# A decoder step on one core: conditioning weights accumulated in PSUM at the start, and the retention's work spread over four engines

## The reference, cut to what matters

```
m = silu(c) @ w_mod + b_mod                      # 6 x 1024 columns, 9 conditioning rows
h = rmsnorm(x, norm1_w) * (1 + sc1) + sh1
z = h @ w_in                                     # rq rk rv rg (4 x 512), mq mk mv (3 x 512)
# retention, 8 heads of 64, chunks of 128 tokens, on rotary q and k
att = (q @ k.T) * dmat
o   = att @ v + (q @ s) * q_dec
s   = s * c_dec + (k * k_dec).T @ v
ret = silu(rg) * ((o - mean(o)) * rsqrt(var(o) + eps) * gn_w)
# block-sparse attention (MoBA): prompt over its own blocks, samples over 3 chosen cache blocks and their own
moba = rmsnorm per head(softmax(q k.T) v)
x = x + g1 * (concat(ret, moba) @ w_out)
x = x + g2 * ((silu(h2 @ w_gate) * (h2 @ w_up)) @ w_down)
```

## Time and profile before

| what | us |
|---|---|
| median of three runs (1113.23 to 1118.26) | 1115.62 |
| the profiled execution, its own time | 1118.47 |
| its span, first to last instruction | 1116.6 |
| PE busy | 979.4 (88%) |
| DVE busy | 656.7 (59%) |
| ACT busy | 339.4 (30%) |
| POOL busy | 91.0 (8%) |
| DMA moved 267.01 MB, mean | 239 GB/s |

### The profile page before, as it was taken

One profiled execution on the slowest core, in us unless ns is written; L12 is line 12 of the kernel. 1 busy time (PEld: TensorE's weight loads), 2 busy tenths in 40 slices (PEclk: granted clock), 3 DMA queues, 4 the chain that ended last, 5 costly groups with the idle time before them and its releaser, 6 DMA issues.

```text
span 1116.6 us, 20916 instructions
## 1 busy us (share of the span) xinstructions
PE 979.4 (88%) x7847; PEld 684.4 (61%) x7847; DVE 656.7 (59%) x1152; ACT 339.4 (30%) x678; POOL 91.0 (8%) x90
## 2 busy tenths in 40 slices
PE   3669999999999657467987699999999999999996
PEld 1356766766776334244753476767677777777775
DVE  3555775676676487776656657543266555553344
ACT  4331233324224324224214414333234222221113
POOL 0011110000010021101400123000000000000000
PEclk8679999999999788787988689999999999999998
DMA  9846878877777768576888567977847798887662
GB/s 294 303 150 232 309 252 280 294 263 265 272 261 261 229 229 307 189 257 208 267 300 281 188 212 249 276 226 227 272 123 216 193 233 236 226 242 237 202 227 80
DMA packets 220355, 267.01 MB, mean 239 GB/s; under 512 B 12785, under 2 KB 175929, under 8 KB 212066
## 3 DMA queue, kind: packets, MB, share of 16 engines
q1 hardware_dynamic: 111586, 123.21, 35.1%
q10 hardware_dynamic: 99456, 75.38, 22.0%
q0 software_dynamic: 9216, 67.11, 16.8%
HBM read 260.04 MB, written 5.64 MB: 238 GB/s over the span
## 4 chain that ended last, share of the span: by engine, by line
PE 73%; DVE 13%; DMA 5%; DVEq 3%; ACT 3%; issue 2%; SPq 1%; ACTq 0%
PE banks L1001 13%; PE banks L1002 12%; PE banks L1003 12%; PE banks L961 6%; PE banks L1016 4%; PE banks L1036 4%; PE banks L1091 4%; DVE KT L1638 4%; PE banks L1017 4%; PE banks L1018 4%; DMA raw<-in_w_mod 2%; PE banks L1179 2%; DVEq L1539 2%; DMA raw<-in_w_out 1%; PE banks L1164 1%
## 5 line engine op out<-in xcount | busy, mean ns | idle before, releaser
L1001 PE MATMUL banks<-ahi,whi 128*128 128x512 f32 x416 | 170.9, 411 | 0.0
L571 ACT ACTIVATE whi<-raw 128x1024 fp32r<-128x1024 f32 (+1 forms) x76 | 78.7, 1035 | 301.3 <-PE banks L1003 157.5
L1638 DVE STREAM_TRANSPOSE KT<-K 128x2048 f32<-128x2048 f32 x64 | 147.7, 2308 | 37.0 <-PE banks L1036 29.7
L1002 PE MATMUL banks<-alo,whi 128*128 128x512 f32 x416 | 164.2, 395 | 0.0
L1003 PE MATMUL banks<-ahi,rawlo 128*128 128x512 f32 x416 | 164.0, 394 | 0.0
L1601 DVE TENSOR_TENSOR rawlo<-raw,whi 128x1024 fp32r<-128x1024 f32 (+1 forms) x76 | 91.4, 1203 | 61.9 <-ACT whi L571 59.1
L478 POOL DMA_INDIRECT K<-in_cache_k,kidx x64 | 64.7, 1011 | 581.8 <-DVE KT L1638 538.2
L1001 PEld LDWEIGHTS banks<-ahi,whi 128*128 128x128 f32 x416 | 79.6, 191 | 31.5 <-issue 13.6
L1036 PE MATMUL banks<-KT,qbd 128*32 128x128 f32 x2048 | 75.2, 291 | 25.5 <-DVE KT L1638 24.2
L1016 PE MATMUL banks<-ahi,whi 128*128 128x512 f32 x224 | 93.6, 418 | 1.2 <-DVE rawlo L1608 0.9
L1003 PEld LDWEIGHTS banks<-ahi,rawlo 128*128 128x128 f32 x416 | 79.3, 191 | 17.7
(11 more groups left out here) (304 smaller groups left out, 1447.6 us busy)
## 6 DMA issues: line engine op xcount, KB each, us to landing
V<-in_cache_v SPq DMA_DIRECT2D x184, 256.0 KB
rawm<-in_w_mod ACTq DMA_DIRECT2D x15, 1024.0 KB
zT<-in_cache_v SPq DMA_DIRECT2D x52, 256.0 KB
raw<-in_w_in ACTq DMA_DIRECT2D x12, 1024.0 KB
raw<-in_w_gate ACTq DMA_DIRECT2D x22, 512.0 KB
raw<-in_w_up ACTq DMA_DIRECT2D x22, 512.0 KB
srw<-in_w_gate SPq DMA_DIRECT2D x22, 512.0 KB, 5.4
srw<-in_w_up SPq DMA_DIRECT2D x22, 512.0 KB, 6.7
```

What stands on the lines that cost most here:

```text
L571: act.activation(whi[t % 2][:, 0:kd, :], raw[u][:, 0:kd, t % 2 * P:(t % 2 + 1) * P], ACT.Copy).then_inc(s_hi, 1)
L1001: pe.matmul(out[:, :], whi[t % 2][:, k, :], hi(k), start=(first and n == 0), stop=False)
L1002: pe.matmul(out[:, :], whi[t % 2][:, k, :], lo(k), start=False, stop=False)
L1638: dve.transpose(KTb[:, :, :, :], Kb[g % 2][:, :]).then_inc(s_kt, 1)
```

## The change

**Start.** The first eight chunks of `w_mod` become eight pieces of two k by 1024 columns, with buffers of their own (`early`, the later `rawm` and `raw`), and x is loaded ahead of them. PE sums each half (four pieces) over k in PSUM in four column groups at once, so that DVE copies 128 x 256 once and adds the bias in two operations instead of folding. The halves are taken one after the other: the gains of k = 0 to 3 come from the first. Of the scaling of x by its root mean square two of four parts go to DVE. Tile 0 and half of tile 1 are placed before `keys(0)`; the order of `mod_chunk` moves one ahead, and the last no longer lies in slot 27.

**Retention.** The cosines, the decay of q and the scaling of three of the four pairs of heads go to POOL, in its queue between two gathers. Centring becomes a product with a matrix `centre` in place of the turning (the same operation on PE turns and centres). ACT squares straight from PSUM and stages the attention's heads; the squares of the attention's heads are accumulated by ACT unit by unit in slots 15 to 29 (32 small operations in all). PE makes k.v for each head alone, 64 columns wide, so that DVE runs the state at 128 rows. `turn_x` is spread, one a slot; the roots are taken one slot earlier. In slot 28 the values are turned earlier and the last unit's probabilities come behind the copies. `slot_rest` on PE is split in `slot_values` and `slot_tail`; their order in each slot comes out as in the kernel before (the tail's products ahead of `weigh` where s % 8 is 4, behind it elsewhere).

**Behind it.** Two waits in the first tile of the output projection move (`last_in`), the units of the feed-forward network lie at other places (`UNIT_AT`) with other waits, and semaphores are merged.

```diff
-MOD_AT = [0, 1] + list(range(2, NT, 2)) + [NT - 1]
-TURN_AT = [2] + [MOD_AT[n] + 2 for n in range(3, len(MOD_AT) - 1, 2)] + [NT]
+MOD_AT = [0, 0, 1] + list(range(2, NT - 1, 2))
+TURN_AT = [s + 2 for s in MOD_AT[1::2]]
...
+    put("centre", np.eye(P) - (p[:, None] // HD == p[None, :] // HD) / HD)
...
+    early = [at(ZT + 8192 + 2048 * i, f"early{i}", [P, 2, DM]) for i in range(3)]
+    two_k = lambda x: x[:, :, :].rearrange("p (k a) c -> p k (a c)", k=2)
+    mod_buffer = early + [two_k(rawm), two_k(raw[0]), two_k(raw[1])] + early[0:2]
+    rawm2 = early[2][:, :, :].rearrange("p k (a c) -> p (k a) c", a=4)
...
+        def early_mod(n):
+            q, i = divmod(n, 4)
+            for a in range(2):
+                cols = slice(a * DM + q * 512, a * DM + q * 512 + 512)
+                sp.dma_start(mod_buffer[n][:, :, a * 512:(a + 1) * 512], w_mod_v[:, 2 * i:2 * i + 2, cols]).then_inc(EARLY[n][0], 16)
...
+        for i in range(TT):
+            sp.dma_start(xP[:, i, :], x_prompt[0, i * P:(i + 1) * P, :]).then_inc(s_x, 16)
+        for n in range(2):
+            early_mod(n)
...
-        sp.dma_start(xP[:, :, :], x_prompt[0].rearrange("(i p) d -> p i d", p=P)).then_inc(s_x, 16)
...
+        for n in range(2, 6):
+            early_mod(n)
+        for n in range(6, NMA):
+            sp.wait_ge(s_md, n - 5)
+            early_mod(n)
+        sp.wait_ge(s_md, 5)
+        chunk(0, w_in_v, slice(COL_OF[0], COL_OF[0] + CHUNK))
+        sp.wait_ge(s_md, 6)
+        chunk(1, w_in_v, slice(COL_OF[1], COL_OF[1] + CHUNK))
+        sp.dma_start(ct[:, P + 40:], const[:, P + 40:NA]).then_inc(s_const, 16)
+        sp.dma_start(rawm[:, :, :], mod_load(0)).then_inc(s_wm, 16)
+        sp.dma_start(rawm2, mod_load(1)).then_inc(s_me[0], 16)
...
+        def cosines(hp):
+            if hp == 0:
+                pool.wait_ge(s_const, 48)
+            for n, sec in enumerate((RK, RQ)):
+                pool.wait_ge(s_rr, 2 * hp + n + 1)
+                pool.tensor_tensor(zT[:, sec + hp, :], zT[:, sec + hp, :], C("cos"), ALU.mult).then_inc(s_rc, 1)
+        def queries_decayed(hp):
+            pool.wait_ge(s_rk, 2 * hp + 2)
+            if hp:
+                pool.wait_ge(s_ro, hp)
+            pool.tensor_tensor(scr[:, 2, :].rearrange("p (c i) -> p c i", c=4), scr[:, 0, :].rearrange("p (c i) -> p c i", c=4),
+                               C("q_dec")[:, hp, :].unsqueeze(1).broadcast_to((P, 4, P)), ALU.mult).then_inc(s_rq, 1)
+        def scale_heads(hp):
+            pool.wait_ge(s_hrs, hp + 2)
+            o = rettok[:, hp, :].rearrange("p (c d) -> p c d", d=HD)
+            pool.tensor_tensor(o, o, gain[:, hp, 0:8].unsqueeze(2).broadcast_to((P, H, HD)), ALU.mult).then_inc(s_hn, 1)
...
+            if g > R_PAIR and (g - R_PAIR - 1) % 3 == 0 and g <= R_PAIR + 10:
+                cosines((g - R_PAIR - 1) // 3)
+            if g > R_PAIR and (g - R_PAIR - 2) % 3 == 0 and g <= R_PAIR + 11:
+                queries_decayed((g - R_PAIR - 2) // 3)
+            if g in (R_PAIR + 7, R_PAIR + 10, R_PAIR + 13):
+                scale_heads((g - R_PAIR - 7) // 3)
+            if g == R_PAIR + 3:
...
+        def unit_squares(n):
+            act.wait_ge(s_on, n + 1)
+            for h2 in range(2):
+                h = 2 * (n % 4) + h2
+                last = act.activation(sq_unit[:, h2, :], mobatok[:, n // 4, h * HD:(h + 1) * HD], ACT.Square,
+                                      accum_out=gain[:, 4 + n // 4, h:h + 1])
+            if n == 15:
+                last.then_inc(s_hsq, 1)
+            act.drain()
...
-            act.activation(rettok[:, hp, :], DB[:, :], ACT.Copy).then_inc(s_roc, 1)
-        def centred_squares(hp):
-            act.wait_ge(s_hc, hp + 1)
-            act.activation(sq_ret[:, :], rettok[:, hp, :], ACT.Square).then_inc(s_hsq, 1)
+            act.activation(rettok[:, hp, :], DB[:, :], ACT.Copy)
+            act.activation(sq_ret[:, :], DB[:, :], ACT.Square).then_inc(s_roc, 1)
...
+        def stage_block_heads(k, n):
+            act.wait_ge(s_xt, n + 1)
+            act.activation(stage[k % 2][:, :], bank[k % 2][:, :], ACT.Copy, scale=vT[:, V_MN + k - 4:V_MN + k - 3]).then_inc(s_stg, 1)
...
+        keep_values(8, rvtok, SB)
+        unit_squares(13)
+        act.wait_ge(s_sc, 16)
+        keep_z(NT - 1)
         probs(15)
-        keep_z(NT - 1)
-        for n in range(8, 12):
-            keep_values(n, rvtok, (DB, SB)[n % 2])
+        for n in range(9, 12):
+            keep_values(n, rvtok, (SB, DB)[n % 2])
         x_in(0)
         slot(NT)
         probs_t(15)
-        act.wait_ge(s_sev, NIN + 2)
-        act.activation(zs[:, ZRG:ZRG + W], zs[:, ZRG:ZRG + W], ACT.Silu).then_inc(s_ssg, 1)
+        unit_squares(14)
         slot(NT + 1)
+        unit_squares(15)
...
+        def slot_rest(s):
+            if s % NGRP == 4:
+                slot_tail(s)
+                slot_values(s)
+            else:
+                slot_values(s)
+                slot_tail(s)
...
+        def early_mod(n):
+            pe.wait_ge(*EARLY[n])
+            for kk in range(2):
+                for g in range(4):
+                    last = pe.matmul(bank[n // 4][32 * g:32 * g + 32, 0:CHUNK], cT[:, 2 * (n % 4) + kk, :],
+                                     mod_buffer[n][:, kk, CHUNK * g:CHUNK * (g + 1)],
+                                     start=(n % 4 == 0 and kk == 0), stop=(n % 4 == 3 and kk == 1))
...
+        for n in range(4):
+            early_mod(n)
+        turn_early(0)
+        pe.wait_ge(s_xsn, 1)
+        for k in range(KT):
+            last = pe.transpose(VO[:, k * S:(k + 1) * S], sq[0:S, k * P:(k + 1) * P], ident[0:S, 0:S])
+        last.then_inc(s_xst, 1)
+        pe.wait_ge(s_xn, 2)
+        turn_x_early(0)
+        turn_x_early(1)
+        early_mod(4)
+        early_mod(5)
+        turn_x_early(2)
+        turn_x_early(3)
+        early_mod(6)
+        turn_x_early(4)
+        turn_x_early(5)
+        early_mod(7)
+        turn_early(1)
+        turn_x_early(6)
+        pe.wait_ge(s_hs, 1)
+        sample_in(0)
+        turn_x_early(7)
+        sample_in(1)
...
+        pe.wait_ge(s_hi, 1)
+        for k in range(KT):
+            pe.wait_ge(s_hlo, k + 1)
+            pe.matmul(DB[:, :], whi[0][:, k, :], ahi[:, k, :], start=(k == 0), stop=False)
+            pe.matmul(DB[:, :], whi[0][:, k, :], alo[:, k, :], start=False, stop=False)
+        pe.wait_ge(s_lo, 1)
+        for k in range(KT):
+            last = pe.matmul(DB[:, :], rawlo[0][:, k, 0:P], ahi[:, k, :], start=False, stop=(k == KT - 1))
+        last.then_inc(s_ft, 1)
+        mod_chunk(0)
+        mod_chunk(1)
+        half_tile(1, 0)
         pe.wait_ge(s_const, 16)
-        for s in range(NT):
+        slot_head(0)
+        half_tile(1, 1)
+        mod_chunk(2)
+        slot_head(1)
+        for s in range(2, NT):
...
-                last = pe.transpose(DB[:, c * P:(c + 1) * P], scr[:, 3, c * P:(c + 1) * P], ident)
+                last = pe.matmul(DB[:, c * P:(c + 1) * P], scr[:, 3, c * P:(c + 1) * P], C("centre"), start=True, stop=True)
...
-                last = pe.matmul(DB[:, c * P:(c + 1) * P], scr[:, 3, c * P:(c + 1) * P],
-                                 rvtok[:, c, hp * P:(hp + 1) * P], start=True, stop=True)
+                for h2 in range(2):
+                    r = 64 * h2
+                    last = pe.matmul(DB[r:r + 64, c * HD:(c + 1) * HD], scr[:, 3, c * P + r:c * P + r + HD],
+                                     rvtok[:, c, hp * P + r:hp * P + r + HD], start=True, stop=True, skip_group_check=True)
             last.then_inc(s_kv, 1)
...
+        def early_modulation(group):
+            dve.wait_ge(s_md, 4 * group + 4)
+            then(cp(mst[:, CHUNK * group:CHUNK * (group + 1)], bank[group][:, 0:CHUNK])).then_inc(s_mev, 1)
+            dve.wait_ge(s_mtp, group + 1)
+            for h in range(2):
+                pick = lambda x: x.rearrange("p (a q k h) -> p a q k h", a=2, q=2, k=2)[:, :, group, :, h]
+                dst = mT[:, 0:16, :].rearrange("p (a q k h) s -> p a q k h s", a=2, q=2, k=2)[:, :, group, :, h, :]
+                last = then(tt(dst, SB[:, h * P:(h + 1) * P].rearrange("p (a k r) -> p a k r", a=2, k=2)[:, :, :, 0:NSEQ],
+                               pick(vT[:, 0:16]).unsqueeze(3).broadcast_to((P, 2, 2, NSEQ)), ALU.add))
+            last.then_inc(s_mp, 1)
...
         def rotated(hp):
+            if hp:
+                dve.wait_ge(s_rq, hp)
+            for n in range(2):
+                dve.wait_ge(s_rr, 2 * hp + n + 1)
+                tt(stage[n][:, :], bank[n][:, :], C("sin"), ALU.mult)
+            dve.drain()
             for n, sec in enumerate((RK, RQ)):
-                dve.wait_ge(s_rr, 2 * hp + n + 1)
...
-                tt(stage[1][:, :], zT[:, sec + hp, :], C("cos"), ALU.mult)
-                then(tt(stage[0][:, :], bank[n][:, :], C("sin"), ALU.mult))
-                then(tt(scr[:, 1 - n, :], stage[1][:, :], stage[0][:, :], ALU.add))
-                dve.drain().then_inc(s_rk, 1)
```

(72 more changed lines are left out.)

456 lines of the change are left out of this document (212 added, 244 removed).

## The result

The changed kernel takes 1077.55 us (median of 4 runs, 1074.34 to 1080.66), the kernel before, run beside it, 1116.94 (1113.23 to 1123.43). The ratio is 0.9641, with a 95% interval of 0.9587 to 0.9695: 39 us less, where 50 were forecast. The profiled execution took 1080.66, its span is 1078.0 (before 1116.6).

A forecast was written before the change was run, and what follows sets the result against it. PE was taken as the bound in most stages; in the start and retention engines wait, DVE and PE alternating in the latter. Start to slot 27 -19, slot 28 -4.5, retention -29, behind +2.5: -50, giving 1067 us, range 1047 to 1091.

The forecast's parts named there:

- The start: Everything until slot 2: weights load at full rate with x ahead, so slot 2 begins near 68.3 instead of 83.5, -15.
- -3 for slot 2's wait for `rawm`: Slot 2 took 11.3 us against slot 3's 7.6; the difference was taken as a wait that earlier loads remove, -3.
- Between, PE is the bound and hands all of it on: Between the start and the retention PE is the bound, so the time won earlier is passed on whole: 0 change.
- The unit squares: ACT's 32 small squares of the attention's heads fall where its load is 86 of 265 us.
- Slots 27 and 28: Slot 27 multiplies one chunk less, -1; slot 28 turns the first value earlier, with no modulation turning ahead of scores, -4.5.
- the 24 us listed: Retention: work leaving DVE, group by group, adds up to 24.3 us, leaving 79 of 103.65.
- the idle time before the second `turn_x`: Retention: PE's 11.7 us wait until ACT copies the bank goes, since the root no longer stands ahead of `keep_x`.
- The undiscounted layout: Retention queues laid out slot by slot from slot 30: slot 43 begins at 483 instead of 520, -37.
- I take three quarters of the -37: Retention: discount because transfers would need 334 GB/s, 93% of full rate; -29 at 309 GB/s, bounds -38 to -17.
- POOL becomes the bound: Retention rival: at 1.75 us each, cosines outlast the sines, and POOL's other work delays output and heads; 1077, chance 0.13.
- Behind it: After the retention, output projection and feed-forward: the queue of transfers is fuller when it begins, +2.5 (0 to +5).
- Tail order: Order of the cache's tail on PE: unchanged by the diff, since the loops give the same order; worth 0.

The follow-up runs named there:

- the second profile: The changed kernel itself, unaltered, run and profiled again to see which slot durations repeat; 1072.03 us, ratio 0.9587 to the kernel before.
- root_late: three_mended with the old order put back for the pair's variance on DVE, ACT's root ahead of `keep_x` and PE's turnings of x; 1073.08 us.
- three_mended: Changed kernel with group 27's value pages waiting one by one, cosines on DVE, and attention heads' small squares moved to just ahead of the exponentials; 1062.57 us.
- tail_first: Changed kernel with the small products of the cache's tail ahead of the weighing of values in every slot; 1076.49 us, ratio 0.9622.

## Why the prediction was right, and where it was off

**The start**, -15 until slot 2: right, 68.3 and 68.28; the second profile had 65.5. The steps on the way are right too: the activations were staged at 47.3 (47 forecast), tile 0 done at 51.7 (53) and `keys(0)` at 58.4 (58.5, though the forecast's own terms, 47 and 10.7, add up to 57.7). The rate up to 40 us was 329 GB/s, and 355 in the second half of that, where near 350 was forecast. That x has to come first is shown by its own run. -3 for slot 2's wait for `rawm` failed: 0.2 came. The wait was a guess from a difference of two slots, and the trace before does not have it:

```profile
83.51:94.85 11.34, 9.77 (x81) 7.02 (x76) 5.39 (x7) 0.71 (x2) 0.94 (x1) 0.85 0.81 286
```

PE was busy for 9.8 of slot 2's 11.3 us, with the products of the modulation and at a mean granted clock of 0.85 (slot 3: 7.58 at 1.00). Its one wait there, 1.6, was for DVE's adding of a chunk. After, it is busy for 9.8 of 11.1 and waits 1.3 ahead of the next chunk; DVE's adding stands behind keys 3, and these are late, in the changed kernel's timeline of DVE:

```profile
73.91 2.31 DVE L1792 STREAM_TRANSPOSE KT<-K 128x2048 f32<-128x2048 f32 x1 [5.68 <-DMA K<-in_cache_k,kidx]
```

The step took a difference for a wait without looking for the wait.

**Slots 3 to 26**, "Between, PE is the bound and hands all of it on": off by +4.8 in the first profile, +7.4 in the second. The unit squares, which the prediction called covered, are covered. What is there is a late value page in one or two slots, 0.7 to 3.7 us each, in the second profile with a spell of PE at its lower clock (1.2 GHz) behind it (mean 0.90 and 0.86 in slots 13 and 14). In the eleven profiles of variants these slots 13 to 26 took 166.9 to 170.8, in the one of before 166.8: whether the changed kernel has more of it than the old one stays open.

**Slots 27 and 28**: right, -0.9 and -4.5.

**The retention.** The mechanism was right in the main: DVE's busy time fell by 21 of the 24 us listed, and the root_late run shows the idle time before the second `turn_x` as an effect of order, 12.3 us with what hangs on it. Of the first, 8.2 us in slot 32, the forecast said that it goes; it went, but another wait of 7.4 us for DVE stands in the same slot, which gave 2.2 us. The undiscounted layout, -37, is near what the program gives with SP's wait mended and the cosines back on DVE: -35.1, each part within 2 us of the layout's. The step that failed is "I take three quarters of the -37", for transfers: three_mended moves 298 GB/s and waits 1.5 us for values. In its place stood 8.4 us of SP's wait on `s_rk` in slot 39 (7.1 against the second profile), which the prediction never looked at, since the diff does not touch it. Some 6 more are mostly scatter: 4.6 of them lie in pair 1, which the second profile of the same program runs through 4.3 us faster, at the higher clock. What POOL's hold on DVE costs the kernel is at most a part of the rest, and no run here shows it. That the discount brought the forecast 8 us nearer to the measured time is luck: its cause was not there, and another loss of that size was. The hold was priced in the wrong column: a cosine took 1.28 (1.1 taken, 0.9 to 1.75 allowed; the row behind the 0.9 had a broadcast operand, and the scalings, which have one too, took 1.05), but the cost showed on DVE, 3.0 us in the eight sums and 3.0 in one scaling of eight columns. Rival "POOL becomes the bound" had the engine right and the mechanism wrong: DVE waited 0.8 us for the cosines' result, and was held the other 6 us while its own operations were running.

**Behind it**, +2.5: -1.9 and -3.2. Slot 43 grew by 3.6, but slot 48 lost a wait of PE that took 4.8 us in the kernel before. **Tail order**, 0: right, since the order did not change; tail_first shows that the other order is worth nothing measurable either.

In the ledger the forecast of -50 missed -38.6 by 11.4: slot 2 2.8, slots 3 to 26 4.8, the retention 8.4 (it fell 14.5 short of the mended kernel, and that 1.9 short of the layout, less the 8 of the discount), behind it -4.4, the start -0.2. The range, 1047 to 1091, held the time.

## What to carry to other kernels

When a stage is shortened, list every wait of a DMA queue on a semaphore of that stage, also the ones that the diff leaves alone: each is a due time that comes nearer, and all that is queued behind it comes with it. Before taking work from an engine, look at the order on the engines around it: of the 35 us to be won here, 13 us of work moved off DVE carried about 2, and the place of one root and of the turnings around it 12; the rest was not taken apart. A difference between two slots is not yet a wait: look for the wait in the trace before it is priced. And a total of one profile is no proof where late transfers and the clock scatter it by 6 us; slots that repeat to 0.03 us are.

## What the runs showed of the hardware

A DVE operation that meets a POOL product of two SBUF operands can wait until that, and what POOL has queued directly behind it, is through: 128x8 took 0.23 us with POOL quiet, 0.81 beside one product of 1.05, and 3.25 to 3.28 in eight runs beside three in a row (3.5 us from the first's start to the third's end). The Trainium skill (SBUF — State Buffer, SBUF: two separate sides) says that DVE and GpSimd share one pair of ports under an exclusive lock, held for the whole instruction, for DVE's 2-port modes or two SBUF inputs; by that rule, the trace agrees for the sums, and products with an operand in PSUM kept 0.69. It agrees for the scaling too if that ran in a 2-port mode, which no row shows. That DVE came in only behind three of POOL's instructions and not behind the first, the page doesn't say; the rows show it.

At the same place of the same program the granted clock can differ from one execution to the next: PE had been idle for 7.4 us in slot 32 of the first profile of the changed kernel and for 8.5 us in the second, and slot 33 then ran at a mean of 0.73 (7.0 us) in the one and at 1.00 (5.4 us) in the other.
